# Zero-padded keys, a local output by key blocks, and moved steps in the attention of a two-model kernel

## What is computed

```python
def second_block(x, ...):
    for l in range(2):
        h = rms_norm_2(x, mix_norm_g[l])
        proj = h @ w_in[l]
        sb_q, sb_k, sb_v, sw_q, sw_k, sw_v, gate_logits = split(proj)
        o_sb = stick_breaking_attention(sb_q, sb_k, sb_v)      # 8 heads of 64
        q = apply_rope(rms_norm_2(sw_q, q_norm_g[l]), cos, sin) # 8 heads of 64
        k = apply_rope(rms_norm_2(sw_k, k_norm_g[l]), cos, sin) # 2 heads of 64
        y_swa = sliding_window_sink_attention(q, k, sw_v, sinks[l]) @ w_branch_swa[l]
        gates = sigmoid(gate_logits)
        x = x + (gates[0] * (o_sb @ w_branch_sb[l]) + gates[1] * y_swa) @ w_out[l]
        x = x + square(relu(rms_norm_2(x, mlp_norm_g[l]) @ w_up[l])) @ w_down[l]

# stick-breaking: z = q k / 8, w_ts = sigmoid(z_ts) * prod_{s<j<t} (1 - sigmoid(z_tj)), s < t only
# local: softmax over keys t-128 < s <= t and one learned sink, blocks of 128 queries and 256 keys
```

## Time and profile before

| | before |
|---|---|
| median of 3 runs | 2821.87 us (2819.51 to 2823.86) |
| profiled execution: its own time | 2823.41 us |
| profiled execution: span, mean granted clock | 2821.9 us, 0.998 |
| PE / PEld busy | 98% / 78% |
| DVE / ACT / POOL busy | 53% / 41% / 4% |
| DMA, mean | 84 GB/s, 16 engines busy about 24% |

### The profile page before, as it was taken

How to read it: one execution, slowest core, us unless ns; L and a number is a source line. 1 busy time by engine, 2 the same in 40 slices (tenths; PEclk the granted TensorE clock), 3 DMA queues, 4 the chain that set the end, 5 groups by cost and what they waited for, 6 DMA issues and landing times.

```text
span 2821.9 us, 30835 instructions
## 1 busy us (share of the span) xinstructions
PE 2757.7 (98%) x12462; PEld 2191.4 (78%) x12462; DVE 1507.7 (53%) x2079; ACT 1163.7 (41%) x1734; POOL 114.4 (4%) x79
## 2 busy tenths in 40 slices
PE   8999999999999999999999999999999999999999
PEld 6788778888887888886666888888866668888887
DVE  4566657465686757575443554443544444544433
ACT  6444344243474424254454333332435443333322
POOL 2333110000010000000000000000000000000000
PEclk9999999999999999999999999999999999999999
DMA  4111112222232222231111222232211112222322
GB/s 172 48 63 50 49 60 105 97 91 101 101 105 103 98 97 98 97 113 67 38 45 38 90 97 97 90 103 97 96 63 45 38 38 92 95 97 90 105 97 75
DMA packets 66956, 235.65 MB, mean 84 GB/s; under 512 B 7552, under 2 KB 8320, under 8 KB 66816
## 3 DMA queue, kind: packets, MB, share of 16 engines
q1 hardware_dynamic: 63504, 228.58, 23.3%
q10 hardware_dynamic: 3312, 5.12, 0.5%
HBM read 231.57 MB, written 2.10 MB: 83 GB/s over the span
## 4 chain that ended last, share of the span: by engine, by line
PE 86%; ACT 6%; DVE 5%; issue 2%; POOL 1%; DMA 0%; SPq 0%; ACTq 0%; DVEq 0%
PE bank L401 25%; PE bank L403 25%; PE bank L402 25%; PE bank L756 1%; PE bank L796 1%; ACT w_hi_k L885 1%; ACT p_t_att L1284 1%; PE bank L745 1%; DVE w_lo_k L1372 1%; DVE p_t_att L1837 1%; PE bank L736 1%; PE bank L808 1%; PE bank L551 1%; PE bank L815 1%; POOL q_mix L1957 1%
## 5 line engine op out<-in xcount | busy, mean ns | idle before, releaser
L401 PE MATMUL bank<-x_hi_k,w_hi_k 128*128 128x512 f32 x2152 | 870.6, 405 | 12.5 <-DVE x_lo_k L1379 11.7
L403 PE MATMUL bank<-x_hi_k,w_lo_k 128*128 128x512 f32 x2152 | 843.1, 392 | 0.0
L885 ACT ACTIVATE w_hi_k<-raw_k 128x1024 fp32r<-128x1024 f32 x431 | 454.4, 1058 | 938.4 <-PE bank L403 936.9
L402 PE MATMUL bank<-x_lo_k,w_hi_k 128*128 128x512 f32 x2152 | 841.3, 391 | 0.0
L1372 DVE TENSOR_TENSOR w_lo_k<-raw_k,w_hi_k 128x1024 fp32r<-128x1024 f32 x431 | 532.6, 1236 | 176.8 <-ACT w_hi_k L885 176.8
L401 PEld LDWEIGHTS bank<-x_hi_k,w_hi_k 128*128 128x128 f32 x2152 | 406.9, 189 | 102.7 <-DVE x_lo_k L1379 14.3
L403 PEld LDWEIGHTS bank<-x_hi_k,w_lo_k 128*128 128x128 f32 x2152 | 405.9, 189 | 87.1
L402 PEld LDWEIGHTS bank<-x_lo_k,w_hi_k 128*128 128x128 f32 x2152 | 406.8, 189 | 83.3 <-issue 4.1
L401 PE MATMUL bank<-y_hi_k,w_hi_k 128*128 128x512 f32 x1136 | 445.0, 392 | 4.5 <-DVE y_lo_k L1700 3.2
L403 PE MATMUL bank<-y_hi_k,w_lo_k 128*128 128x512 f32 x1136 | 442.2, 389 | 0.0
L402 PE MATMUL bank<-y_lo_k,w_hi_k 128*128 128x512 f32 x1136 | 442.1, 389 | 0.0
(11 more groups left out here) (320 smaller groups left out, 2564.4 us busy)
## 6 DMA issues: line engine op xcount, KB each, us to landing
raw_k<-wstream SPq DMA_DIRECT2D x431, 512.0 KB, 3.2
outT<-h_k ACTq DMA_DIRECT2D x8, 256.0 KB, 2.8
h_k<-xT SPq DMA_DIRECT2D x4, 256.0 KB, 7.9
h_k<-xT ACTq DMA_DIRECT2D x4, 256.0 KB, 7.4
decay_mix<-constants ACTq DMA_DIRECT2D x4, 256.0 KB, 2.6
levels_mix<-constants SPq DMA_DIRECT2D x1, 448.0 KB, 10.8
vec_k<-vectors SPq DMA_DIRECT2D x1, 282.5 KB, 9.3
cos_mix<-constants SPq DMA_DIRECT2D x1, 256.0 KB, 9.9
```

The source lines that it names most:

```text
L401: pe.matmul(dst, wh, rh, start=start, stop=False)
L402: pe.matmul(dst, wh, rl, start=False, stop=False)
L403: return pe.matmul(dst, wl, rh, start=False, stop=stop)
L885: act.activation(k.w_hi[:, u % SPLIT, :], k.raw[:, u % RAW, :], ACT.Copy).then_inc(*hi_done.mark())
```

## The change

Keys of a head no longer lie in 64 rows beside the other head's. For each half there is a copy of 128 rows in which the other head's rows are zero (`zk` for the stick-breaking keys, `zwk` for the local keys), so that the products contract over 128 rows and take the full query tile. Zeros are written once (four memsets on DVE before the last feed-forward part of the first model); the copy of k at a pair's start becomes two copies of 64 rows, and the scaling of the local keys, once a layer, becomes two instructions. To make room, `w_t` holds one half instead of two, and `wk` shares its place with `wq`.

The local output is summed by blocks of keys: four products of 256, 256, 256 and 128 columns take the place of seven of 128 (the probabilities of one key block for its own and for the next query block lie side by side).

The squares for the next pair's queries are made by ACT at the end of a pair, for the first pair of a layer where they were. The window task gets one more step in each half, between scores and transposes (21 steps become 23), and ends at 0.9 of a pair.

```diff
-    k.sp_t, k.w_t = take("sp_t", [P, KEYS]), take("w_t", [P, 2, KEYS])
+    k.sp_t, k.w_t = take("sp_t", [P, KEYS]), take("w_t", [P, KEYS])
+    k.wk = k.wq
+    k.zk, k.zwk = take("zk", [P, 2, T]), take("zwk", [P, 2, T])
...
-WINDOW_STEPS = 6 + 2 * 7 + 1
+WINDOW_STEPS = 6 + 2 * 8 + 1
...
-    return ((stick, STICK_STEPS, 0, 1), (window, WINDOW_STEPS, 0, 0.85),
+    return ((stick, STICK_STEPS, 0, 1), (window, WINDOW_STEPS, 0, 0.9),
...
+def head_rows(half):
+
+    return slice(half * 64, half * 64 + 64), slice(64 - half * 64, 128 - half * 64)
...
-            pe.matmul(z_view(k, j), k.ak[r, j * P:j * P + P], k.aq[r, j * P:T], start=True, stop=False)
+            pe.matmul(z_view(k, j), k.zk[:, half, j * P:j * P + P], k.aq[:, j * P:T], start=True, stop=False)
...
-                    mm = pe.matmul(s[:, P:2 * P], k.wq[r, 0:P], k.wk[r, 0:P], start=False, stop=True)
+                    mm = pe.matmul(s[:, P:2 * P], k.wq[:, 0:P], k.zwk[:, half, 0:P], start=False, stop=True)
                 else:
                     pe.matmul(s, k.id_b[:], k.mask_b[:, 2 * P:4 * P], start=True, stop=False)
-                    mm = pe.matmul(s, k.wq[r, n * P:n * P + P], k.wk[r, (n - 1) * P:(n + 1) * P],
+                    mm = pe.matmul(s, k.wq[:, n * P:n * P + P], k.zwk[:, half, (n - 1) * P:(n + 1) * P],
                                    start=False, stop=True)
             mm.then_inc(*mark("scores", *at, half))
+            yield
...
             pe.wait_ge(*act_done.at("pT", *at, half))
+            seen = k.pT[:].rearrange("p n s -> p (n s)")
             for n in range(TC):
-                if n > 0:
-                    pe.matmul(bank[6][r, n * P:n * P + P], k.wvt[:, n - 1, r], k.pT[:, n, 0:P], start=True, stop=False)
-                mm = pe.matmul(bank[6][r, n * P:n * P + P], k.wvt[:, n, r], k.pT[:, n, P:2 * P], start=n == 0,
-                               stop=True)
+                to = min((n + 2) * P, T)
+                mm = pe.matmul(bank[6][r, n * P:to], k.wvt[:, n, r], seen[:, (2 * n + 1) * P:(n + 1) * P + to],
+                               start=n == 0, stop=n == 3, skip_group_check=True)
...
+    def window_squares(layer, m):
+        act.wait_ge(*dve_done.at("fill", UNIT["pair", layer, m, 3]))
+        act.activation(k.sq, k.lands[3][:], ACT.Square).then_inc(*mark("wq_sq", layer, m))
...
         act.activation(k.y_hi[:, pair, :], k.ao[:], ACT.Copy).then_inc(*mark("att_y", layer, pair))
+        if pair < 3:
+            window_squares(layer, pair + 1)
 
     def window(layer, m):
         at = (layer, m)
-        act.wait_ge(*dve_done.at("fill", UNIT["pair", layer, m, 3]))
-        act.activation(k.sq, k.lands[3][:], ACT.Square).then_inc(*mark("wq_sq", *at))
+        if m == 0:
+            window_squares(layer, 0)
...
+    for half in range(2):
+        r, other = head_rows(half)
+        dve.memset(k.zk[other, half, :], 0.0).then_inc(*mark())
+        dve.memset(k.zwk[other, half, :], 0.0).then_inc(*mark())
     conv_ffn(1, "final", "norm_final", 0)
...
-        dve.tensor_copy(k.ak[:], k.lands[1][:]).then_inc(*mark("qk", *at))
+        for half in range(2):
+            r, other = head_rows(half)
+            mm = dve.tensor_copy(k.zk[r, half, :], k.lands[1][r, :])
+            mm.then_inc(*(mark("qk", *at) if half else mark()))
...
-        dve.tensor_scalar(k.wk[:], k.wk[:], 0.125, None, ALU.mult).then_inc(*mark("wk", layer))
+        for half in range(2):
+            r, other = head_rows(half)
+            mm = dve.tensor_scalar(k.zwk[r, half, :], k.wk[r, :], 0.125, None, ALU.mult)
+            mm.then_inc(*(mark("wk", layer) if half else mark()))
```

More of the change, by code:

```diff
@@ L289, in attention_memory @@
     k.lands = [take(n, [P, T]) for n in ("land_q", "land_k", "land_v", "land_w")]
-    k.aq, k.ak, k.ao = [take(n, [P, T]) for n in ("q", "k", "o")]
+    k.aq, k.ao = [take(n, [P, T]) for n in ("q", "o")]
     k.vt = take("vt", [P, TC, P])
     k.e_t = take("e_t", [P, 2, T])
-    k.sp_t, k.w_t = take("sp_t", [P, KEYS]), take("w_t", [P, 2, KEYS])
-    k.wk, k.wq, k.wo = [take(n, [P, T]) for n in ("wk", "wq", "wo")]
+    k.sp_t, k.w_t = take("sp_t", [P, KEYS]), take("w_t", [P, KEYS])
+    k.wq, k.wo = [take(n, [P, T]) for n in ("wq", "wo")]
+    k.wk = k.wq
     k.rot = Arena(k.nc, "att", k.ssum_at).take("rot", [P, T])
@@ L730, in logits @@
         def logits(n, half, j):
-            r = slice(half * 64, half * 64 + 64)
             if n == 0:
@@ L755, in output @@
             for s in range(TC):
-                mm = pe.matmul(bank[5][r, s * P:T], k.vt[:, s, r], keys_view(k.w_t[:, half, :], s), start=s == 0,
+                mm = pe.matmul(bank[5][r, s * P:T], k.vt[:, s, r], keys_view(k.w_t, s), start=s == 0,
                                stop=s == TC - 1)
@@ L1256, in stick @@
                 act.wait_ge(*pe_done.at("log_w", *at, n - 1))
-                act.activation(keys_view(k.w_t[:, half, :], s), z_view(k, s),
+                act.activation(keys_view(k.w_t, s), z_view(k, s),
                                ACT.Exp).then_inc(*mark("weights", *at, n - 1))
```

## The result

The changed kernel takes 2806.82 us (median of four runs, 2806.18 to 2807.28), the kernel before beside it 2822.86 (2819.51 to 2826.43): a ratio of 0.9941, 95% interval 0.9929 to 0.9954. The gain of 16 to 17 us has the forecast sign and the time lies inside the range (2787 to 2812), but above the likeliest 2799 and above the narrower 2794 to 2804 that was given 0.58. The profiled execution takes 2806.42 us, against 2823.4 before: 17.0 less.

The account below looks back on a forecast made before the run. PE, busy 98% of the span, was taken to bound the kernel. Shorter pairs (61.2 against 63.91 us) give 21.3 us and the clock 3.0: 2823.4 - 21.3 - 3.0 = 2799, range 2787 to 2812.

Parts of the forecast that it names:

- Row groups of 64: PE's logits and scores: padding to 128 rows saves 0.29 us per logits product, 1.05 per scores group, 4.4 a pair.
- A: Rival: second weight load stays uncovered, 0.1 us per fp32 product, some 1.4 a pair, 2810 us; chance 0.08.
- B: Rival: excess belongs to the fp32 product beside a bf16 mask product and stays; slower, 2829 us; chance 0.04.
- T to the first logits: From the v transposes to the first logits: 3.64 us, with PE idle some 2.2 us for DVE's copies.
- Logits to S: First logits to first head's scores: 6.8 us through activation, softplus and rotation; about 1.5 us new wait for rotated queries.
- S to P: First head's scores to its transposes: about 14.5 us against 13.92 before; old wait for probabilities about gone.
- P to the next T: First head's transposes to next pair's v transposes: 39.38 - 4.4 + 1.4 = 36.3 us.
- The sum: Whole pair: 61.2 us against 63.91, 2.7 less in six pairs, 2.53 in two, 21.3 us in all.
- rival E: DVE or ACT is late by 1 us a pair more than counted: 2807 us; chance 0.14.
- C: Rival: clock falls at 16 further new waits, 1.7 us each, +27, 2826 us; chance 0.04.
- D: Rival: wait for second head's copies hidden, 2788 us, or the one before the first scores, 12 less; chance 0.12.
- Clock: PE's slowed stretches: 4.3 us before; four or five of eight pairs at 0.3 each, 1.3 after; minus 3 us.

Follow-up runs that it names:

- early copies: Changed kernel with DVE's copies of the next pair's queries and keys at a pair's end, except for a layer's first pair: 2799.9 us, ratio 0.9922.
- the sums first: Changed kernel with DVE's sums over keys ahead of the reciprocal and probability multiplies in the second head: 2799.3 us, ratio 0.9917.
- after: The changed kernel itself, against the kernel before: 2806.82 us, ratio 0.9941.
- swapped part: Changed kernel with the window's last step due at 0.898 instead of 0.9, second head's transposes one part earlier: 2796.9 us, ratio 0.9907.
- three edits: Changed kernel with early copies, the sums first and the window's last step due at 0.898 of a pair: 2785.9 us, ratio 0.9868.
- 64 rows again: Changed kernel with logits and scores formed from the head's 64 rows alone: 2845.4 us, ratio 1.0085.

## Why the prediction was right, and where it was off

- **Row groups of 64**: right. 0.29 for one product of the logits (measured 1.20 against 0.91) and 1.05 for a scores group (3.07 to 2.0). Rivals A and B fell with it.
- **T to the first logits**: 0.11 off. The two 64-row copies were put at 0.34 + 0.42; they take 0.87:

```profile
1430.83 0.42 DVE L1788 COPY q_att<-land_q_att 128x512 f32<-128x512 f32 x1
1431.16 0.87 DVE L1791 COPY zk_att<-land_k_att 64x512 f32<-64x512 f32 x2
1432.08 0.49 PE L742 MATMUL bank<-q_att,zk_att 128*128 128x128 f32 x2 [2.29 <-DVE zk_att L1791]
1432.41 0.22 PE L743 MATMUL bank<-mask_b_att,id_b_att 128*128 128x128 bf16 x1
```

- **Logits to S**: 6.90 instead of 6.8. The mask product follows the first logits by 0.33 (1432.08 to 1432.41), not the 0.22 of the sum. The wait before S is 1.4, as forecast 1.5. The early copies showed that the chain named there sets S.
- **S to P**: 14.49 for 14.47. But no term of the sum asked what the pair would be without the moved steps; with the padding alone this stretch is 12.79 and the pair shorter.
- **P to the next T**: this step failed, 37.20 for 36.3. The wait of 1.3 for the copies of probabilities was right. What was missed is the wait for the sums, for which the forecast has no term: `log_weights` of 384 columns (L751) waits for the sums of 128 columns that DVE makes behind the softplus, and in DVE's queue these stood behind the four multiplies. 1411.13 to 1412.14 is 1.01 us where 0.23 would do: 0.78 of the 0.9. The kernel with the sums first got 0.86 of it back.
- **The sum**: 1.56 a pair instead of 2.7 is 8.8 us too much gain; the clock gave 0.7 back and the earlier start 0.8, which leaves the 7.3 between 2799.1 and 2806.4. Those 1.5 us are luck. The time was closest to rival E (1 us a pair later by DVE or ACT, 2807), with another cause than lateness: an order. Rivals C (the clock falls behind the new waits as well) and D (a wait is hidden) didn't come: no stretch in after costs more than 0.36 us, and all the new waits are in the list.
- **Clock**: minus 3.0 forecast, minus 3.7 measured in attention. The cost before was 4.2, not the forecast's 4.3. Four stretches of eight pairs were forecast (or five), and the profiled execution has four, all ahead of S. Each costs 0.36 (pair 1) or 0.03 (pairs 3, 4 and 7), where 0.3 was forecast, since PE then waits less for the rotated queries. The premise that a piece of idle time of 2.2 us makes stretches likelier isn't borne out: the kernel with the sums first and the one with the swapped part both have that wait of 2.3 us in all eight pairs. The windows view over all of attention, of the first and then of the second, gives a granted clock of 1.00 for the one and less for the other, and a single stretch of the other shows 0.50:

```profile
1304.43:2330.00 1025.57, 985.47 (x4366) 756.88 (x4365) 470.59 (x715) 431.89 (x782) 0.00 (x0) 1.00 0.22 71
```
```profile
1304.29:2330.00 1025.71, 998.04 (x4380) 763.87 (x4379) 472.26 (x716) 433.84 (x785) 0.00 (x0) 0.99 0.21 71
```
```profile
1490.92:1494.33 3.41, 3.21 (x9) 2.67 (x10) 1.39 (x4) 0.90 (x3) 0.00 (x0) 0.50 0.51 159
```

The second has five such stretches, the first none. In the same way the kernels with early copies and with three edits (above) both wait about 2.5 us ahead of S in six pairs, and the first has one stretch behind S, the second four. So such a piece of idle time doesn't decide it.
- **Squares and output**: costed at nothing in the sum and found at 0.04 a pair together.

What stays open is what decides whether a slowed stretch falls into a pair. With it goes 0.5 us of the time of after, some 4 of before, 6.6 of the kernel with three edits and 12 of the one with 64 rows again.

## To carry over

A product that uses half the rows cost its columns and, among full ones, 0.29 us more here. Where such products stand among full ones, pad with zeros: the columns stay the same, and the price here was room for the padded tiles and one more copy at a pair's start. Each change between half and full rows that goes is a gain, so a group that alternates brings most. Before moving steps to hide a wait, time the plain edit alone: here the waits that the moved steps removed were cheaper than those that they made. For each step moved, list every semaphore of each waiting instruction, and for each its producer's place in its own queue; the one missed here was the sums, behind 1.1 us of multiplies that nobody wanted yet. And work that stands ahead of a place set by another engine is free there and nowhere else.

## What the runs showed of the hardware

The 64-row excess is 0.29 us for one logits product among 128-row products (1.20 against 0.91), and the same 0.29 for each output of 256 columns in a group that alternates with 128-row masks (0.84 against 0.55). Weight loads ran under a product on the same 128 rows (after, 1379.82 and 1380.38) and not across a change between 64 and 128 rows (the kernel with the logits over 64 rows, 1317.79 and 1318.63). Two copies of 512 columns over 64 rows took 0.87 us on DVE, one over 128 rows 0.42. Slowed stretches came in lengths of 3.41 us and, in the kernel with 64 rows again, of 10.24. They cost 0.03 to 0.7 us where a wait of PE follows, 1.4 to 1.7 where none does, and 4.7 for the long one.
